# Unread matmuls on TensorE between the last down quarters of each layer and ahead of layer 1's first norm

## The chip, the cores and the metric

The kernel runs on one core of a Trainium2 chip. The metric is the time of one execution on the device in microseconds. Three runs of the kernel before gave 1234.24, 1233.4 and 1233.99 us, median 1233.99.

## The reference

A trunk of two decoder layers over 256 tokens of width 1024, all in float32. Layer 0 mixes tokens with retention and HGRN2, layer 1 with stick-breaking and differential attention. Behind each mixer stands a mixture of experts with two levels of routing.

```python
for l in range(DEPTH):
    h = rms_norm(x, norm_mix[l])
    if l % 2 == 0:
        mix = retention_hgrn2_mixer(h, w_in_ab[j], w_out_ab[j], ...)
    else:
        mix = stickbreak_diff_mixer(h, w_in_cd[j], w_out_cd[j], ...)
    x = x + mix
    h = rms_norm(x, norm_ffn[l])
    x = x + hierarchical_moe(h, ..., w_gate[l], w_up[l], w_down[l])

def expert_block(args):          # 32 experts a layer, top 2 for each token
    xb, e = args
    a = jax.nn.silu(xb @ w_gate[e]) * (xb @ w_up[e])
    return a @ w_down[e]
```

## The kernel before, in words

Every engine runs a program of its own, written out by hand, and they meet at semaphores. SyncE (SP) issues the loads. Weights come in units of 2 MB (128 partitions x 4096 floats) into eleven places, six in `ring` and five in `wide`. A place is loaded again when TensorE has counted up `unit_used` for the unit that lay there, so SP follows TensorE by that one counter.

A layer's mixer projects the normed input with `w_in` (`project`, L759 with a 512 wide moving operand, L756 with a 256 wide one), attends, and multiplies by `w_out` (L806). Ahead of layer 1's mixer TensorE transposes the normed tokens (`turn_h`, L701, 8 transposes for each half of the tokens), VectorE and ScalarE copy them to `hT` (L735), and the first projection begins.

The experts of a layer are worked through in 8 quads of 4 experts. A quad has three matrices, gate, up and down, four units each, and `matrix` (L531) multiplies them: four experts stand side by side in the array, each with 32 columns of weights (the tokens that chose it), and 512 columns of expert weights stream past. A float32 matmul leaves two records in the trace. In between, `gather` (L487) picks the tokens of the next quad, and `spread_back` (L494, 4 matmuls, 8 records) adds the outputs of the quad before to the sums in PSUM banks 0 to 3. The last down matrix of a layer (quad 7, matrix 2) is loaded in another cut: its four units are quarters, unit q holding chunk q of all four experts, and TensorE waits for a quarter (`wait_unit`), does its 8 matmuls, and goes to the next. The order on TensorE at a layer's end is thus: the last up matrix, the transposes L558 and L560, four quarters of down, and, after VectorE and ScalarE have copied the result out (L640, L592), the last `spread_back`. VectorE adds it to `x` (L643). Then every engine looks at a flag (`over_i`, L835 on TensorE) for whether some expert had more tokens than its 32 slots, and branches; with these inputs that work is passed over.

Behind layer 0, ScalarE squares `x` (L673), VectorE finds the root (L655 to L658) and applies the norm (L689, one instruction for each half of the tokens), and TensorE's transposes for layer 1 wait for each half. Bank 5 of PSUM, `UP`, holds the product with the up matrix, and later the turned weights that ScalarE copies to `spread` (L590).

Of the kernel before, what the change touches and what calls it, by code (L numbers as in the profile page):

```python
# [24 lines left out]
SEQ = 256  # L25
# [104 lines left out]
def build(nc, t, where, const_width, stop_after=4):  # L130
    with ExitStack() as ctx:
# [16 lines left out]
        psum = ctx.enter_context(nc.psum_tensor("psum", [P, 8, 512], F32))  # L148
# [15 lines left out]
        def const(name):  # L164
            a, b = where[name]
            if b <= KEPT_CONSTS:
                return consts[:, a:b]
            tables, start = (masks0, KEPT_CONSTS) if b <= LAYER1_CONSTS else (masks1, LAYER1_CONSTS)
            return tables[:, a - start:b - start]

        ident, before, from_on = const("ident"), const("before"), const("from_on")
        ones = const("ones")
# [94 lines left out]
        def moe_base(layer):  # L267
            return unit_base(layer) + UNITS_IN[layer] + UNITS_OUT

        def unit_place(layer, n):  # L270

            l, m, place = in_turn[unit_base(layer) + n]
            assert (l, m) == (layer, n)
            return place

        def expert_unit(layer, u):

            return UNITS_IN[layer] + UNITS_OUT + u
# [6 lines left out]
        def unit_landings(layer, n):  # L285

            place = unit_place(layer, n)
            return 16 * sum(in_turn[i][2] == place for i in range(unit_base(layer) + n + 1))
# [5 lines left out]
        def slot(layer, n):  # L294

            place = unit_place(layer, n)
            return ring[:, place, :] if place < RING else wide[:, (place - RING) * UNIT:(place - RING + 1) * UNIT]

        def group_buffer(b):

            return ring[:, 2 * b:2 * b + 2, :].rearrange("p u (h n) -> p (u h) n", n=HALF)

        def wait_unit(eng, layer, n):
            eng.wait_ge(unit_landed[unit_place(layer, n)], unit_landings(layer, n))
# [158 lines left out]
        ACC, GATE, UP, YB = 0, 4, 5, 6  # L463
# [8 lines left out]
        def start_sums(pe, layer, rnd):  # L472

            pe.wait_ge(M[layer]["y_ready"], 2 * (rnd * (QUADS + 1) + 1))
            for b in range(4):
                pe.matmul(psum[:, ACC + b, :], spread[:, 0, :], y_sb[:, 0:512], start=True, stop=False,  # L476
                          skip_group_check=True)

        def moe_pe(pe, layer, over, rnd):
            m = M[layer]  # L480
            n17, n16 = rnd * (QUADS + 1), rnd * QUADS
            mb = moe_base(layer)

            def gather(chunks=KC):
                for c in range(chunks):
                    for tc in range(TC):
                        mm = pe.matmul(psum[:, YB + c // 4, (c % 4) * P:(c % 4 + 1) * P], h[:, tc, c, :],  # L487
                                       sel[:, tc, :], start=tc == 0, stop=tc == TC - 1)
                mm.then_inc(m["gathered"], 1)

            def spread_back():
                for tc in range(TC):
                    for n in range(2):
                        mm = pe.matmul(psum[:, ACC + 2 * tc + n, :], spread[:, tc, :],  # L494
                                       y_sb[:, 512 * n:512 * (n + 1)], start=False, stop=False,
                                       skip_group_check=True)
                mm.then_inc(m["spread_done"], 1)

            def over_matrix(i, matrix, out, inp, rows, width):

                for j in range(2):
                    b = (2 * matrix + j) % OVER_BUFFERS
                    pe.wait_ge(over_landed[layer, b], (((rnd - 1) * QUADS + i) * (GROUPS // OVER_BUFFERS)
                                                       + ((2 * matrix + j) // OVER_BUFFERS + 1)) * 16)
                    w = group_buffer(b).rearrange("p e (c n) -> p e c n", n=width)
                    for k in range(rows // 2):
                        c = j * (rows // 2) + k
                        for n in range(width // 512):
                            for e in range(TILE):
                                slots = slice(e * SLOTS, (e + 1) * SLOTS)  # L510
                                mm = pe.matmul(psum[slots, out + n, :], inp[:, c, slots], w[:, e, k, 512 * n:512 * (n + 1)],
                                               start=c == 0, stop=c == rows - 1)
                    mm.then_inc(m["used"], 1)

            def matrix(i, matrix, out, inp, rows, width):

                if over:
                    return over_matrix(i, matrix, out, inp, rows, width)
                units = [expert_unit(layer, i * PER_QUAD + matrix * TILE + j) for j in range(TILE)]
                quartered = (i, matrix) in QUARTERED  # L520
                per = rows // 4
                for c in range(rows):
                    if quartered and c % per == 0:
                        wait_unit(pe, layer, units[c // per])
                    for n in range(width // 512):
                        for e in range(TILE):
                            if not quartered and c == 0 and n == 0:
                                wait_unit(pe, layer, units[e])
                            slots = slice(e * SLOTS, (e + 1) * SLOTS)
                            unit, at = (units[c // per], (e * per + c % per) * width) if quartered else (units[e], c * width)  # L530
                            mm = pe.matmul(psum[slots, out + n, :], inp[:, c, slots],  # L531
                                           slot(layer, unit)[:, at + 512 * n:at + 512 * (n + 1)],
                                           start=c == 0, stop=c == rows - 1)
                            if not quartered and c == rows - 1 and n == width // 512 - 1:
                                mm.then_inc(S["unit_used"], 1)
                    if quartered and (c + 1) % per == 0:
                        mm.then_inc(S["unit_used"], 1)

            if over:
                start_sums(pe, layer, rnd)  # L540
            pe.wait_ge(m["sel_ready"], n17 + 1)
            pe.wait_ge(S["normed"], TC * (2 * layer + 2))
            gather()
            if not over:
                pe.wait_ge(S["route_ready"], layer + 1)

            def quad(i, last=False):
                pe.wait_ge(m["xT_ready"], n17 + i + 1)
                matrix(i, 0, GATE, xT, KC, FF)
                pe.wait_ge(m["y_ready"], 2 * (n17 + i + 1))  # L550
                spread_back()
                matrix(i, 1, UP, xT, KC, FF)

                pe.wait_ge(m["sel_ready"], n17 + i + 2)
                gather(1 if last else KC)
                pe.wait_ge(m["act_ready"], n16 + i + 1)
                for c in range(FC):
                    pe.transpose(psum[:, GATE, c * P:(c + 1) * P], act_h[:, c, :], ident)  # L558
                for tc in range(TC):
                    mm = pe.transpose(psum[:, UP, tc * P:(tc + 1) * P], selw[:, tc, :], ident)  # L560
                mm.then_inc(m["turned"], 1)
                pe.wait_ge(m["actT_ready"], n16 + i + 1)
                pe.wait_ge(m["xT_ready"], n17 + i + 2)
                matrix(i, 2, YB, actT, FC, D)
            if over:
                with pe.Fori(0, QUADS) as i:
                    quad(i)
            else:
                for i in range(QUADS):
                    quad(i, last=i == QUADS - 1)  # L570
            pe.wait_ge(m["y_ready"], 2 * (n17 + QUADS + 1))
            spread_back()

        def moe_act(act, layer, over, rnd):
            m = M[layer]
# [1050 lines left out]
```

## Time and profile before

| | |
|---|---|
| median of three runs | 1233.99 us |
| profiled execution | 1239.58 us, span 1237.8 us |
| TensorE (PE) busy | 957.2 us, 77% of the span |
| VectorE (DVE) busy | 244.8 us, 20% |
| ScalarE (ACT) busy | 133.0 us, 11% |
| read from HBM | 446.47 MB, 362 GB/s over the span |
| mean granted TensorE clock | 0.879 of full speed |

The table is of one profiled execution. It shows no engine busy all the time; what bounds a stretch has to be read from the stretch itself. The granted clock is given as a share of full speed: 1.00 is 2.4 GHz and 0.50 is 1.2 GHz.

### The profile page before, as it was taken

How to read it: one execution, taken by the hardware profiler on the slowest of the kernel's cores; microseconds unless marked ns; L12 is line 12 of the kernel's file. 1: busy time of each engine (PE TensorE's matmuls, PEld its weight loads, DVE VectorE, ACT ScalarE, POOL GpSimd, SP SyncE). 2: the span in 40 equal slices, each digit the busy share in tenths (PEclk: the TensorE clock that was granted, in tenths of full speed). 3: DMA queues.
4: the chain of work that ended last, by engine and by line, in shares of the span. 5: the costliest groups of instructions: out<-in, count | busy, mean ns of one | idle time of the engine just before them, and what ended most of it. 6: DMA issues, size and time to landing. Idle time of an engine off the chain costs nothing.

```text
span 1237.8 us, 11947 instructions
## 1 busy us (share of the span) xinstructions
PE 957.2 (77%) x5092; PEld 403.6 (33%) x5092; DVE 244.8 (20%) x664; ACT 133.0 (11%) x228; POOL 9.9 (1%) x10
## 2 busy tenths in 40 slices
PE   5999999776776858576759999896767677585775
PEld 4645554221212212131225755532121212121211
DVE  3622333110101010110134441511000000010101
ACT  3401211000000000000011331110000000000000
POOL 0000010000000000000000000000000000000000
PEclk9999999987878878787979999998788788887878
DMA  9773396999999999999995327799999999999994
GB/s 325 242 264 134 143 429 279 429 429 426 428 428 427 426 430 427 428 428 426 412 387 188 126 79 281 317 428 429 429 425 429 427 429 427 428 427 429 426 421 196
DMA packets 62149, 448.32 MB, mean 362 GB/s; under 512 B 13072, under 2 KB 13328, under 8 KB 39568
## 3 DMA queue, kind: packets, MB, share of 16 engines
q1 hardware_dynamic: 62096, 447.53, 87.5%
q8 instruction: 43, 0.70, 0.2%
q14 instruction: 10, 0.08, 0.0%
HBM read 446.47 MB, written 1.05 MB: 362 GB/s over the span
## 4 chain that ended last, share of the span: by engine, by line
DMA 50%; PE 45%; DVE 2%; SPq 1%; issue 1%; ACT 1%; DVEq 0%; ACTq 0%
PE psum L531 17%; DMA ring<-in_w_up 15%; PE psum L759 11%; DMA ring<-in_w_down 10%; DMA wide<-in_w_gate 10%; DMA wide<-in_w_down 9%; DMA ring<-in_w_gate 5%; PE psum L756 5%; PE psum L806 4%; PE psum L487 1%; PE psum L494 1%; PE psum L476 1%; SPq L337 1%; PE psum L701 1%; DMA x<-in_x 0%
## 5 line engine op out<-in xcount | busy, mean ns | idle before, releaser
L531 PE MATMUL psum<-ring,mixed 128*32 128x512 f32 x1664 | 400.7, 704 | 128.2 <-DMA ring<-in_w_up 57.2
L531 PE MATMUL psum<-wide,mixed 128*32 128x512 f32 x1408 | 402.8, 721 | 110.8 <-DMA wide<-in_w_gate 61.4
L531 PEld LDWEIGHTS psum<-ring,mixed 128*32 128x32 f32 x1664 | 92.1, 127 | 331.4 <-issue 162.0
L531 PEld LDWEIGHTS psum<-wide,mixed 128*32 128x32 f32 x1408 | 88.5, 129 | 273.7 <-issue 120.3
L759 PE MATMUL psum<-ring,wide 128*128 128x512 f32 x320 | 142.3, 600 | 1.3 <-DVE wide L735 1.3
L759 PEld LDWEIGHTS psum<-ring,wide 128*128 128x128 f32 x320 | 60.4, 193 | 72.0 <-issue 70.2
L635 DVE TENSOR_TENSOR mixed<-psum,sig 128x512 f32<-128x512 f32 x16 | 16.9, 1057 | 279.2 <-PE psum L531 279.2
L494 PE MATMUL psum<-y_sb,spread 128*128 128x512 f32 x144 | 66.6, 605 | 1.6 <-DVE y_sb L640 1.6
L487 PE MATMUL psum<-sel,h 128*128 128x128 f32 x520 | 62.8, 279 | 3.5 <-DVE sel L608 3.5
L487 PEld LDWEIGHTS psum<-sel,h 128*128 128x128 f32 x520 | 59.4, 192 | 17.1 <-issue 13.4
L756 PE MATMUL psum<-wide,ring 128*128 128x256 f32 x256 | 59.7, 395 | 1.4 <-DVE wide L735 1.4
L632 DVE TENSOR_TENSOR sig<-psum,sig 128x512 f32<-128x512 f32 x16 | 11.1, 691 | 238.4 <-ACT sig L585 238.4
L579 ACT COPY mixed<-psum 128x1024 f32<-128x1024 f32 x18 | 18.2, 1012 | 354.9 <-PE psum L487 354.9
L756 PEld LDWEIGHTS psum<-wide,ring 128*128 128x128 f32 x256 | 50.2, 198 | 10.1 <-DVE wide L735 1.8
L640 DVE COPY y_sb<-psum 128x512 f32<-128x512 f32 x16 | 11.1, 691 | 197.9 <-PE psum L531 197.9
L616 DVE TENSOR_SCALAR selw<-consts,rank,wtab 128x32 f32<-128x32 f32 x144 | 31.4, 295 | 50.6 <-PE psum L560 50.5
L494 PEld LDWEIGHTS psum<-y_sb,spread 128*128 128x128 f32 x144 | 25.9, 189 | 43.7 <-issue 39.2
L585 ACT ACTIVATE sig<-psum 128x512 f32<-128x512 f32 x16 | 9.6, 597 | 254.7 <-PE psum L531 254.7
L592 ACT COPY y_sb<-psum 128x512 f32<-128x512 f32 x16 | 9.4, 585 | 210.1 <-PE psum L531 210.1
L608 DVE TENSOR_SCALAR sel<-consts,rank,small 128x32 f32<-128x32 f32 x144 | 31.3, 294 | 0.1
L806 PE MATMUL psum<-ring,y_sb 128*128 128x512 f32 x64 | 28.4, 594 | 0.4 <-ACT small L1044 0.4
L806 PE MATMUL psum<-ring,wide 128*128 128x512 f32 x64 | 27.8, 592 | 0.0
(243 smaller groups left out, 468.4 us busy)
## 6 DMA issues: line engine op xcount, KB each, us to landing
ring<-in_w_down SPq DMA_DIRECT2D x38, 2048.0 KB, 34.8
ring<-in_w_up SPq DMA_DIRECT2D x36, 2048.0 KB, 38.3
wide<-in_w_gate SPq DMA_DIRECT2D x34, 2048.0 KB, 36.1
ring<-in_w_gate SPq DMA_DIRECT2D x30, 2048.0 KB, 30.8
wide<-in_w_up SPq DMA_DIRECT2D x28, 2048.0 KB, 28.3
wide<-in_w_down SPq DMA_DIRECT2D x26, 2048.0 KB, 35.5
ring<-in_w_in_ab SPq DMA_DIRECT2D x8, 2048.0 KB, 15.2
ring<-in_w_in_cd SPq DMA_DIRECT2D x6, 2048.0 KB, 20.4
```

Source lines behind the costliest of these rows:

```text
L337: sp.dma_start(dst_cols(slot(layer, n)), src).then_inc(unit_landed[unit_place(layer, n)], 16)
L476: pe.matmul(psum[:, ACC + b, :], spread[:, 0, :], y_sb[:, 0:512], start=True, stop=False, skip_group_check=True)
L487: mm = pe.matmul(psum[:, YB + c // 4, (c % 4) * P:(c % 4 + 1) * P], h[:, tc, c, :], sel[:, tc, :], start=tc == 0, stop=tc == TC - 1)
L494: mm = pe.matmul(psum[:, ACC + 2 * tc + n, :], spread[:, tc, :], y_sb[:, 512 * n:512 * (n + 1)], start=False, stop=False, skip_group_check ...
L531: mm = pe.matmul(psum[slots, out + n, :], inp[:, c, slots], slot(layer, unit)[:, at + 512 * n:at + 512 * (n + 1)], start=c == 0, stop=c == ...
L579: nc.scalar.copy(xT, psum[:, YB:YB + 2, :].rearrange("p b (c s) -> p (b c) s", s=P)).then_inc(m["xT_ready"], 1)
L608: r = nc.vector.tensor_scalar(sel[:, tc, e * SLOTS:(e + 1) * SLOTS], const("iota"), rank[:, tc, bass.ds(quad * TILE + e, 1)], small[:, 2 + ...
L616: r = nc.vector.tensor_scalar(selw[:, tc, e * SLOTS:(e + 1) * SLOTS], const("iota"), rank[:, tc, bass.ds(quad * TILE + e, 1)], wtab[:, tc, ...
L635: nc.vector.tensor_tensor(act_h.rearrange("p c s -> p s c"), psum[:, UP, :].rearrange("p (s c) -> p s c", c=FC), sig.rearrange("p (s c) -> ...
L756: mm = pe.matmul(banks[:, m // 2, (m % 2) * SEQ:(m % 2 + 1) * SEQ], w[:, c, m * P:(m + 1) * P], hT[:, c, :], start=c == 0, stop=c == KC - 1)
L759: mm = pe.matmul(banks[:, m, :], hT[:, c, m * P:(m + 1) * P], w[:, c, :], start=c == 0, stop=c == KC - 1)
L806: mm = pe.matmul(psum[:, OUT_BANK[layer] + 2 * tc + n, :], mixT(half)[:, c, tc * P:(tc + 1) * P], w[:, c, 512 * n:512 * (n + 1)], start=ha ...
```

## The change

A new function in `moe_pe`, `stay_warm(times)`, issues matmuls of the 128x128 identity with a 128x256 table of ones, into bank 5 (`UP`). Nothing reads what they write, and no semaphore stands on them. They are issued at two places:

- in `matrix`, for the last down matrix of a layer: 6 of them before the waits for quarters 1, 2 and 3, so 18 a layer, in both layers;
- in `moe_pe`, behind the last `spread_back` of layer 0: 20 of them, ahead of the look at the flag.

The first quarter of quad 0's gate matrix is cut in quarters too, but is excluded by `matrix == 2`.

```diff
+            def stay_warm(times):
+
+                for _ in range(times):
+                    pe.matmul(psum[:, UP, 0:SEQ], ident, ones, start=True, stop=True, skip_group_check=True)
+
             def over_matrix(i, matrix, out, inp, rows, width):
...
                     if quartered and c % per == 0:
+                        if matrix == 2 and c:
+                            stay_warm(6)
                         wait_unit(pe, layer, units[c // per])
...
             pe.wait_ge(m["y_ready"], 2 * (n17 + QUADS + 1))
             spread_back()
+            if layer == 0 and not over:
+                stay_warm(20)
```

TensorE's order at the end of layer 0 before, from the last transposes to the flag. `mixed` is the turned activation, the `wide` operand the down weights, and `unit_landed6` to `unit_landed9` are the landings of quarters 0 to 3:

```order
L560 MATMUL psum<-consts,selw 128x128 x2
L531 MATMUL psum<-wide,mixed 32x512 [waits unit_landed6,moe0_xT_ready,moe0_actT_ready]
L531 MATMUL psum<-wide,mixed 32x512 x7
L531 MATMUL psum<-wide,mixed 32x512 [waits unit_landed7]
L531 MATMUL psum<-wide,mixed 32x512 x7
L531 MATMUL psum<-wide,mixed 32x512 [waits unit_landed8]
L531 MATMUL psum<-wide,mixed 32x512 x7
L531 MATMUL psum<-wide,mixed 32x512 [waits unit_landed9]
L531 MATMUL psum<-wide,mixed 32x512 x7
L494 MATMUL psum<-y_sb,spread 128x512 [waits moe0_y_ready]
L494 MATMUL psum<-y_sb,spread 128x512 x3
```

And the same place now (the lines of the file have moved: L531 is L538, and L502 is the new matmul):

```order
L538 MATMUL psum<-wide,mixed 32x512 x7
L502 MATMUL psum<-consts 128x256 x6
L538 MATMUL psum<-wide,mixed 32x512 [waits unit_landed7]
L538 MATMUL psum<-wide,mixed 32x512 x7
L502 MATMUL psum<-consts 128x256 x6
L538 MATMUL psum<-wide,mixed 32x512 [waits unit_landed8]
L538 MATMUL psum<-wide,mixed 32x512 x7
L502 MATMUL psum<-consts 128x256 x6
L538 MATMUL psum<-wide,mixed 32x512 [waits unit_landed9]
L538 MATMUL psum<-wide,mixed 32x512 x7
L494 MATMUL psum<-y_sb,spread 128x512 [waits moe0_y_ready]
```

Each group of six now stands in TensorE's order between one quarter's matmuls and the next quarter's wait; nothing else changed place. Behind the last `spread_back` of layer 0 stands now, on TensorE, the group of 20 and then the read of the flag:

```order
L494 MATMUL psum<-y_sb,spread 128x512 x3
L502 MATMUL psum<-consts 128x256 x20
L844 TENSOR_LOAD over_i
L844 ISA x2
L844 COMPARE_AND_BRANCH
```

Before, the read of the flag came directly behind `spread_back`:

```order
L494 MATMUL psum<-y_sb,spread 128x512 [waits moe0_y_ready]
L494 MATMUL psum<-y_sb,spread 128x512 x3
L835 TENSOR_LOAD over_i
L835 ISA x2
L835 COMPARE_AND_BRANCH
```

The other engines' orders are as they were.

## Rows read from the trace of the kernel before

**Rows 1.** The page's chain that ended last: shares of the span by engine.

```profile
DMA 50%; PE 45%; DVE 2%; SPq 1%; issue 1%; ACT 1%; DVEq 0%; ACTq 0%
```

**Rows 2.** The chain in order of time: start us, us, what.

```profile
596.59 24.05 DMA wide<-in_w_down
...
641.93 1.24 DVE wide L735
```

**Rows 3.** Timeline of TensorE, end of layer 0: start us, us, group [idle before].

```profile
611.71 3.64 PE L531 MATMUL psum<-wide,mixed 128*32 128x512 f32 x32 [0.95 <-ACT spread L590]
615.56 1.92 PE L531 MATMUL psum<-wide,mixed 128*32 128x512 f32 x16 [0.21 <-DMA wide<-in_w_down]
620.68 3.38 PE L531 MATMUL psum<-wide,mixed 128*32 128x512 f32 x16 [3.20 <-DMA wide<-in_w_down]
624.89 3.70 PE L494 MATMUL psum<-y_sb,spread 128*128 128x512 f32 x8 [0.82 <-DVE y_sb L640]
638.10 3.79 PE L701 MATMUL psum<-consts,h 128*128 128x128 f32 x16 [9.51 <-DVE h L689]
643.21 2.08 PE L759 MATMUL psum<-ring,wide 128*128 128x512 f32 x2 [1.32 <-DVE wide L735]
```

**Rows 4.** Timeline of TensorE, end of layer 1: its four down quarters.

```profile
1212.61 3.64 PE L531 MATMUL psum<-wide,mixed 128*32 128x512 f32 x32 [0.95 <-ACT spread L590]
1216.67 1.92 PE L531 MATMUL psum<-wide,mixed 128*32 128x512 f32 x16 [0.42 <-DMA wide<-in_w_down]
1221.68 3.26 PE L531 MATMUL psum<-wide,mixed 128*32 128x512 f32 x16 [3.08 <-DMA wide<-in_w_down]
```

**Rows 5.** Windows of TensorE: from:to, us, busy (records), clock, DMA share, GB/s.

```profile
612.00:617.00 5.00, 4.79 (x48) 1.00 1.02 409
...
620.50:623.50 3.00, 2.82 (x16) 0.50 1.05 387
624.50:628.50 4.00, 3.61 (x8) 1.00 1.05 388
...
634.00:638.00 4.00, 0.00 (x0) 0.50 1.05 381
...
643.00:647.00 4.00, 3.79 (x5) 0.50 1.05 388
648.00:652.00 4.00, 4.00 (x11) 1.00 1.05 391
```

**Rows 6.** The chain in order of time: two stretches of projection at full clock.

```profile
77.56 13.73 PE psum L759 x32
...
673.97 13.82 PE psum L756 x64
```

**Rows 7.** Timeline of weight loads (PEld), start of layer 1's first projection.

```profile
646.78 0.34 PEld L759 LDWEIGHTS psum<-ring,wide 128*128 128x128 f32 x1 [0.52 <-issue]
647.61 0.19 PEld L759 LDWEIGHTS psum<-ring,wide 128*128 128x128 f32 x1 [0.49 <-issue]
```

**Rows 8.** Timeline of TensorE, where the weights go between 32 and 128 columns.

```profile
589.82 0.59 PE L531 MATMUL psum<-wide,mixed 128*32 128x512 f32 x1
590.35 3.70 PE L494 MATMUL psum<-y_sb,spread 128*128 128x512 f32 x8
...
593.98 1.05 PE L531 MATMUL psum<-ring,mixed 128*32 128x512 f32 x4
```

**Rows 9.** Timeline of VectorE, from the end of layer 0 to the norm.

```profile
632.17 0.06 DVE L1481 MEMSET small<- 128x1 f32 x1 [1.20 <-issue]
...
636.07 3.79 DVE L689 SCALAR_TENSOR_TENSOR h<-x,small,wide 128x1024 f32<-128x1024 f32 x2
```

**Rows 10.** Timeline of TensorE, behind layer 1's mixer: transposes and router.

```profile
778.19 1.09 PE L709 MATMUL psum<-consts,x 128*128 128x128 f32 x8 [0.44 <-DVE x L1216]
779.12 3.88 PE L821 MATMUL psum<-rw,wide 128*128 128x36 f32 x32
```

**Rows 11.** Windows of TensorE over the same place, columns as in Rows 5.

```profile
777.00:783.00 6.00, 5.52 (x47) 1.00 1.01 430
784.00:787.00 3.00, 3.00 (x4) 0.52 1.02 437
```

**Rows 12.** Waits of SP's queue from 640 to 850 us: us in total, times, longest.

```profile
SPq L337 <- PE psum L759: 64.7, 4, 20.0
```

## The prediction

> **What bounds the kernel now.** I read the chain that ended last first. Half of the span is DMA and 45% TensorE [rows 1]: the experts' weights stream, and the mixers and what lies between them are TensorE's. The change touches two kinds of place only, so I went along the chain to those. At the end of layer 0 it runs over the load of the last down quarter [rows 2], over that quarter's matmuls, and the same at the end of layer 1.
>
> Then the timeline of TensorE at these ends. Quarters 0 and 1 have landed when TensorE comes to them and run as one block of 32 records, quarter 2 waits 0.21 us, and only quarter 3 waits long, 3.20 us [rows 3]. Layer 1 ends in the same way, with waits of 0.42 and 3.08 us [rows 4]. The granted clock is 1.00 up to the end of quarter 2 and 0.50 in quarter 3, where TensorE had stood still before it; it is back at 1.00 for `spread_back` [rows 5]. So the half clock costs at an end the difference between a quarter of 3.38 or 3.26 us and one of 1.92 us, about 1.4 us, and nothing behind it.
>
> After layer 0's last `spread_back` TensorE stands still for 9.51 us, until the first half of the norm is there [rows 3]. The clock is down at 634 us, and is still down when the projection begins at 643.21 us; it rises near 647.6 us, where the weight loads go from 0.34 to 0.19 us [rows 5, 7].
>
> **The price of one unread matmul.** It has a 256 wide moving operand, as L756 has, whose 64 records take 13.82 us at full clock [rows 6]: 0.216 us a record, two records a matmul, so 0.432 us. Six are 2.59 us, eighteen 7.78, twenty 8.64.
>
> **The ends of the layers.** The point is where the six stand. They are done whether the next quarter has landed or not. Before quarters 1 and 2 there is next to nothing to wait for, so these twelve push everything back, and the wait before quarter 3 is only some 3 us long.
>
> Layer 0, from the start of quarter 0 at 611.71 us: a quarter's 16 records stream in four groups of 0.43 us (0.43 is the pitch of the 32 records of L759 in 13.73 us [rows 6]), 1.72 us, four quarters 6.88 us, with 0.2 us until the last is out (1.92 less 1.72), 7.08 us. The eighteen add 7.78 us. Each time the weights change between 32 and 128 columns there is a small loss: L494 starts 0.53 us after the record of L531 before it, where 0.43 is the pitch, so 0.10 us; and its eight records, streaming until 590.35 + 8 x 0.43 = 593.79 us, are followed by L531 at 593.98 us, so 0.19 us [rows 8]. Three groups in between make 3 x 0.29 = 0.87 us. Sum 15.73 us: quarter 3 ends at 627.44 us instead of 620.68 + 3.38 = 624.06 us. That is 3.38 us later. All quarters have landed long before their turn (quarter 3 at 620.68 us, its turn is 627.44 - 1.92 = 625.5 us), so the wait that is to be covered is gone, the clock stays up, and the end is late all the same, because TensorE's own queue is late now.
>
> Layer 1: 1212.61 + 15.73 = 1228.34 us against 1221.68 + 3.26 = 1224.94 us, 3.40 us later. Together +6.8 us. The bounds: with no loss at the switches +2.5 us an end, 5.0 in all; with the loss half as large again, 3.8 us an end, 7.6 in all. I take 6.8, since the rows have both directions of the switch.
>
> What waits behind: VectorE's and ScalarE's copies of the result (L640, L592), then `spread_back`, the addition to `x`, and in layer 0 the norm, in layer 1 the output. Nothing beside them hides it. Of SP's queue in layer 1's first half I looked at whom it waits for: TensorE's projections above all [rows 12], so its loads for the next experts move with TensorE, and a delay or a gain at layer 1's start goes through to the end. The first two units of layer 1 are in time: the loads run at 388 GB/s throughout [rows 5] and the second is needed a projection later (13.73 us [rows 6]).
>
> **The start of layer 1.** Taken in the times of before, the twenty begin when `spread_back` has streamed, 624.89 + 8 x 0.43 = 628.33 us, and are out at 636.97 us. The transposes can start at 638.10 us at the earliest. So they fit, with 1.1 us to spare. Behind them TensorE reads the flag and branches, which has cost VectorE 1.20 us [rows 9]; even if TensorE begins that only when it has run dry, it is ready at 638.2 us, and the 0.1 us is lost in the pause before the second half of the transposes, which waits for the norm until 636.07 + 3.79 = 639.9 us. So nothing is added here.
>
> What can be won: the second eight transposes at full clock take 1.09 us [rows 10], so end at 641.0 instead of 641.89 us, 0.9 us. The projection runs cold from 643.21 to 647.61 us, 4.40 us for about 5.2 records of 0.85 us, which at 0.43 us take 2.2 us: 2.2 us more. In all 3.1 us, if the clock is still up after the pause of 1.1 us, the transposes, the pause between their halves, and the copy of 1.24 us [rows 2]. The other end is 0: the clock falls in that stretch, and the projection is as cold as before.
>
> The nearest place is behind layer 1's mixer: two bursts of transposes with pauses and small router matmuls, 777 to 783 us, at 1.00 throughout, and then 0.52 in the window after a pause of one us [rows 10, 11]. So a stretch of transposes and pauses holds the clock for some time, but six us of thin work ended at the half clock. Ours, from 637.0 to about 642.3 us, is a little shorter, with nothing between the transposes. I take 2.2 us, between the 0 and the 3.1, nearer to the upper end because the clock did hold in the row as long as transposes were in it.
>
> The Trainium skill has a rule that speaks against this (TensorE: Matmul & The Clock Gate, Part 4: PE-mode transpose): the full clock does not engage for transposes, since they don't count as busy in the way that matmuls do. By it the twenty would buy nothing, and the sum would be 6.8. Against it stands the window from 777 us at 1.00 with sixteen transposes in or just ahead of it [rows 11], which it doesn't foresee unless the router's matmuls count; so I leave it as a rival.
>
> **Sum.** +6.8 - 2.2 = +4.6 us on the profiled execution's 1239.58 us, 1244.2 us. The profiled execution is 5.6 us above the median of the runs shown, 1233.99 us; I carry the difference over unchanged: 1238.6 us, 0.4% slower.
>
> **The rivals.**
>
> 1. The clock does not last until the projection. The fall in the row at 784 us speaks for it. At most the second transposes gain. +6.8 - 0 to 0.9: 1239.9 to 1240.8 us, say 1240.5. Slower too. The change then does not do what its second part says.
>
> 2. The overrun is about as large as the gain. The switches cost nothing, since weights may be loaded ahead of the quarter, and the full 3.1 us come in: +5.0 - 3.1 = +1.9 us, 1235.9 us. Or a matmul of the identity costs half the price, 0.216 us: eighteen are 3.89 us, quarter 3 ends at 611.71 + 7.08 + 3.89 + 0.87 = 623.55 us, 0.5 us early at each end, but then the twenty are out at 632.7 us, long before the norm, and win nothing: -1.0 us, 1233.0 us. For it speaks nothing in the rows but that these operands do not occur in them.
>
> 3. Faster. Without the profiler the last quarters land later in relation to TensorE, so that the eighteen lie in a wait that is longer. Every us of that takes one us from each overrun. With the full 3.1 us of layer 1 it decides from 3.1 us on: 6.8 - 2 x 3.1 - 3.1 = -2.5 us, 1231.5 us; and if quarter 3 is 4.8 us later, so that it is just in time for its turn at 625.5 us, the warm quarter saves 1.4 us at each end, 1228 us. Against it: the two ends agree with each other within 0.2 us in all their waits, [rows 3, 4], and the quarters' landings are 5.1 and 5.0 us apart in both, which is the rate of the loads.
>
> **How the numbers follow.** Overrun at both ends and a gain of 1 to 3.1 us (1237.7 to 1239.8 us): 0.55. Rival 1: 0.25. Rival 2: 0.14. Rival 3: 0.06. A change of this kernel can be told from none from about 0.2%, 2.5 us, on: the forecast and rival 1 are slower by more, with a little of the forecast's lower edge lost: slower 0.81; within 0.2% rival 2 and part of rival 3, 0.14; faster 0.05. The range reaches from below 1235.9 us, the case of free switches, to 1241.6, which is the dear switches (7.6) without a gain: 1235.5 to 1241.6 us.
>
> **What would show it.** At both ends TensorE should be busy from quarter 0 to quarter 3 with no wait for `wide<-in_w_down`, the clock at 1.00 throughout, quarter 3 at 1.92 us, and its end 15.7 us after quarter 0's start. L502 should have 112 records, those of a group 0.216 us apart. The idle time before the transposes of layer 1 should fall from 9.51 to about 1.1 us. In the projection the weight loads of 0.34 us should be gone (forecast) or about five (rival 1). If quarter 3 still waits for its load, or the records of L502 are closer than 0.2 us, the first term is wrong and the time falls towards 1233.

## The result and the profile after

The changed kernel takes 1246.24 us (median of four runs, 1244.9 to 1247.13) against 1233.7 us, ratio 1.0098 with a 95% interval of 1.0081 to 1.0114. It is slower by 12.5 us; 4.6 were forecast, and the time lies outside the range.

Between the two profiled executions there are only 5.3 us (1244.9 against 1239.58). The profile after is 1.3 us below the median of its own kernel's runs; the one of before, on which the prediction rests, was 5.6 us above the median of its runs. Part of that is seen in the chain of waits. This is the chain of after, in order of time (start us, us, what):

```profile
16.67 27.89 PE psum L765 x128
...
642.14 1.98 PE psum L710 x16
...
645.42 27.73 PE psum L768 x64
...
1230.34 0.70 DVE y_sb L649
```

The first projection of layer 0 took 27.89 us here and 30.93 us in the profile of before, though nothing was changed there. The absolute times of the two profiles therefore can't be set against each other; distances inside a stage can. TensorE's timeline at the end of layer 0 after, columns as in [rows 3]:

```profile
597.13 9.97 PE L538 MATMUL psum<-ring,mixed 128*32 128x512 f32 x58 [3.86 <-DMA ring<-in_w_up]
...
610.06 1.92 PE L538 MATMUL psum<-wide,mixed 128*32 128x512 f32 x16 [0.95 <-ACT spread L599]
611.91 2.86 PE L502 MATMUL psum<-consts 128*128 128x256 f32 x12
614.70 1.92 PE L538 MATMUL psum<-wide,mixed 128*32 128x512 f32 x16
...
623.98 1.92 PE L538 MATMUL psum<-wide,mixed 128*32 128x512 f32 x16
626.72 3.70 PE L494 MATMUL psum<-y_sb,spread 128*128 128x512 f32 x8 [0.81 <-DVE y_sb L649]
630.26 8.80 PE L502 MATMUL psum<-consts 128*128 128x256 f32 x40
642.14 1.97 PE L710 MATMUL psum<-consts,h 128*128 128x128 f32 x16 [3.09 <-DVE h L698]
645.42 14.86 PE L768 MATMUL psum<-ring,wide 128*128 128x512 f32 x34 [1.32 <-DVE wide L744]
```

The tail is what was forecast: no wait for a down quarter is left, a quarter is 1.92 us, and quarter 3 ends 623.98 + 1.92 - 610.06 = 15.84 us after quarter 0's start (forecast 15.73). Until VectorE copies the result, at 625.97 us, it is 15.91 us, and 15.92 in layer 1. The windows (from:to, us, busy, clock, DMA share, GB/s) answer [rows 5]:

```profile
610.00:626.00 16.00, 15.85 (x100) 1.00 1.04 394
...
639.00:642.00 3.00, 0.05 (x1) 1.00 1.05 383
642.50:645.00 2.50, 1.60 (x15) 1.00 1.05 386
645.50:649.00 3.50, 3.50 (x9) 1.00 1.03 384
```

The clock is up from quarter 0 to the projection, as intended (1.00 in the windows between these too). But before the transposes TensorE stands still for 3.09 us behind the last of the twenty, where 1.1 us was forecast. VectorE's own row says that it is TensorE that is late:

```profile
637.91 3.79 DVE L698 SCALAR_TENSOR_TENSOR h<-x,small,wide 128x1024 f32<-128x1024 f32 x2
```

The first half of the norm, for which the first transposes wait, was ready near 639.9 us, the second at 641.7, and the transposes began at 642.14.

So the profile after confirms the work at the tail and shows one cost that was not foreseen. It does not show where the other 7 us of the 12.5 come from. For that the kernel before had to be seen in a usual execution.

### The profile page after: what moved, and what is told of

The parts are those of the page before. It is cut to its first block, busy times and chain, and to the rows that moved or that the text cites. A ratio compares the mean times of both kernels' runs of the same rounds, so it can differ in the third digit from the quotient of the medians.

```text
span 1243.0 us, 12171 instructions
## 1 busy us (share of the span) xinstructions
PE 979.8 (79%) x5204; PEld 423.4 (34%) x5204; DVE 245.0 (20%) x664; ACT 133.1 (11%) x228; POOL 9.9 (1%) x10
## 4 chain that ended last, share of the span: by engine, by line
DMA 48%; PE 47%; DVE 3%; issue 1%; ACT 1%; DVEq 0%; ACTq 0%
PE psum L538 18%; DMA ring<-in_w_up 13%; PE psum L768 11%; DMA wide<-in_w_gate 10%; DMA wide<-in_w_down 10%; DMA ring<-in_w_down 5%; DMA ring<-in_w_gate 5%; DMA wide<-in_w_up 5%; PE psum L765 5%; PE psum L815 4%; PE psum L502 1%; PE psum L487 1%; PE psum L494 1%; PE psum L476 1%; DVE h L698 0%
## 5 line engine op out<-in xcount | busy, mean ns | idle before, releaser
L538 PE MATMUL psum<-ring,mixed 128*32 128x512 f32 x1664 | 407.2, 715 | 123.2 <-DMA ring<-in_w_up 53.1
L538 PE MATMUL psum<-wide,mixed 128*32 128x512 f32 x1408 | 402.4, 712 | 105.1 <-DMA wide<-in_w_gate 62.9
L538 PEld LDWEIGHTS psum<-ring,mixed 128*32 128x32 f32 x1664 | 92.9, 128 | 326.0 <-issue 161.2
L538 PEld LDWEIGHTS psum<-wide,mixed 128*32 128x32 f32 x1408 | 88.2, 127 | 267.3 <-issue 122.3
L765 PE MATMUL psum<-wide,ring 128*128 128x256 f32 x256 | 56.7, 381 | 1.4 <-DVE wide L744 1.4
## 6 DMA issues: line engine op xcount, KB each, us to landing
ring<-in_w_gate SPq DMA_DIRECT2D x30, 2048.0 KB, 30.9
```

What stands on the lines that cost most here:

```text
L538: mm = pe.matmul(psum[slots, out + n, :], inp[:, c, slots], slot(layer, unit)[:, at + 512 * n:at + 512 * (n + 1)], start=c == 0, stop=c == ...
L765: mm = pe.matmul(banks[:, m // 2, (m % 2) * SEQ:(m % 2 + 1) * SEQ], w[:, c, m * P:(m + 1) * P], hT[:, c, :], start=c == 0, stop=c == KC - 1)
```

## The experiments

Ratios are to the kernel before, whose median was 1233.1 to 1233.7 us in these comparisons; behind each stands its 95% interval. A diff that takes out or alters `stay_warm` is against the changed kernel, one that adds a loop of matmuls is against the kernel before, and the last one against the run with twelve and fourteen. "To the copy" is the distance from the start of down quarter 0 to VectorE's copy of the result (L640).

### The kernel before, seen again

> The kernel before, unchanged, as a second profile of it. The profiled execution of before (1239.58 us) lay 5.6 us above its timed runs, while that of after (1244.9) lay at the lower edge of its runs. Theory P (the clock's phase): the granted clock rises and falls at other moments of the program from one execution to the next, and the first profile of before met an unlucky start (clock up at 22.9 us, 3 us of extra time in the first projection). Then this profile is near 1234 us, with the projection L756 x128 in the chain near 28 us instead of 30.93, and the last up matrices of 8.5 or 9.9 us depending on where the rise falls. Theory S: the profiled execution is slower by itself; then 1239 to 1240 again with 30.9 us there. Ratio 1.000 either way.

Measured: 1232.22 us, 0.9998 (0.9976 to 1.0019), profile 1235.91 us. First the last up matrix in the first profile, from its second block on, which [rows 3] leaves out:

```profile
600.24 8.51 PE L531 MATMUL psum<-ring,mixed 128*32 128x512 f32 x58 [3.85 <-DMA ring<-in_w_up]
```

And the timeline of TensorE at the ends of layer 0 and, in the last line, of layer 1 in the second profile:

```profile
601.81 9.70 PE L531 MATMUL psum<-ring,mixed 128*32 128x512 f32 x58 [3.87 <-DMA ring<-in_w_up]
...
614.46 5.36 PE L531 MATMUL psum<-wide,mixed 128*32 128x512 f32 x48 [0.95 <-ACT spread L590]
622.26 1.92 PE L531 MATMUL psum<-wide,mixed 128*32 128x512 f32 x16 [2.44 <-DMA wide<-in_w_down]
625.00 3.70 PE L494 MATMUL psum<-y_sb,spread 128*128 128x512 f32 x8 [0.81 <-DVE y_sb L640]
638.21 3.52 PE L701 MATMUL psum<-consts,h 128*128 128x128 f32 x16 [9.51 <-DVE h L689]
643.05 3.27 PE L759 MATMUL psum<-ring,wide 128*128 128x512 f32 x7 [1.32 <-DVE wide L735]
...
1219.29 1.92 PE L531 MATMUL psum<-wide,mixed 128*32 128x512 f32 x16 [2.28 <-DMA wide<-in_w_down]
```

Set beside [rows 3] three things differ. Quarter 3 runs at full clock, 1.92 us instead of 3.38. The last up matrix's second block takes 9.70 us, where it took 8.51 in the first profile: more of it is at the half clock, so quarter 0 starts later in relation to the loads and the copy is reached 9.80 us after it, not 12.43. And the projection of layer 1 is warm without any unread matmuls. The windows show the clock:

```profile
602.00:606.00 4.00, 4.00 (x20) 0.50 1.03 410
...
620.00:622.00 2.00, 0.00 (x0) 1.00 1.04 397
622.50:626.00 3.50, 2.69 (x19) 1.00 1.05 389
634.00:637.00 3.00, 0.00 (x0) 0.50 1.05 384
...
638.00:641.00 3.00, 2.79 (x13) 0.50 1.05 386
641.00:642.00 1.00, 0.73 (x5) 0.85 1.05 385
642.00:643.00 1.00, 0.00 (x0) 1.00 1.06 391
643.00:647.00 4.00, 3.95 (x9) 1.00 1.05 386
```

From the up matrix's second block to the landing of quarter 3 it is 622.26 - 601.81 = 20.45 us here and 620.68 - 600.24 = 20.44 us in the first profile. The loads set that, not TensorE. A slower up matrix comes out of the wait for quarter 3, and behind the shorter wait the clock is still up. Layer 1's end is alike (9.64 us to the copy). The sixteen transposes begin at 0.50 behind 9.51 us of standing still, and the clock rises within them (0.85 in the window from 641 us), so that the projection finds it up; in the first profile the same transposes stayed at 0.50.

The first projection took 29.52 us in the chain, between the expected values. Theory P holds: two executions of one program differ in where the clock changes. Theory S falls: of the fourteen profiled executions of this document six lie below the median of their kernel's runs, by 1.2 to 3.6 us.

> The kernel before, unchanged, one more look, to see how often its last quarter runs cold. In its first profile it took 3.38 and 3.26 us behind a wait of 3.2 us, in the second 1.92 us at both ends behind a wait of 2 us, after a last up matrix of 9.6 to 9.8 us instead of 8.4. Theory A (the time that a half clock costs in the last up matrix comes out of the wait for quarter 3, so from up's second block to the landing of quarter 3 there are always 20.4 us): again 20.4 us, and either a short up with a cold quarter or a long up with a warm one. If the first profile was typical: both ends 12.4 us from quarter 0 to the copy.

Measured: one profile, 1236.26 us. 20.45 us again in layer 0 and 20.92 in layer 1, the up block 9.80 and 9.92 us, quarter 3 1.92 us at both ends, 9.67 and 10.04 us to the copy. Over all nine profiles of kernels without unread matmuls at the tails there are 18 layer ends. In 15 the up block took 9.6 to 10.0 us, the wait before quarter 3 was 2.0 to 2.7 us and the quarter 1.92 us. In 3 the up block took 8.35 to 8.51 us, the wait was 3.1 to 3.2 us and the quarter was cold; two of these are the first profile's. From up's second block to the landing it is 20.3 to 20.5 us in 17 of the 18, and why it was 20.92 once is open.

### The tails alone

In all four of these the twenty are left out.

```diff
-            if layer == 0 and not over:
-                stay_warm(20)
```

> Only the three groups of six unread matmuls before quarters 1, 2, 3 at both layers' ends; the twenty are left out. My sum: +3.4 to 3.5 us at each end. Layer 1's start as before (transposes and projection cold). So +7 us, 1241 us. Rival (the twenty cost the rest): the same +7 here, and the twenty add 5. Rival (the tails cost more in the timed runs than in the profile, because the quarters land earlier or the clock never fell there): +9 to +12 here.

Measured: 1245.71 us, 1.0102 (1.0069 to 1.0135), 12 us slower; 15.92 us to the copy at both ends. The last rival is met: the tails are the loss of 12.5 us to within the noise. The distance from the up matrix's second block to the copy shows how: in the second profile of before it is 22.45 and 22.44 us, after the change 625.97 - 597.13 = 28.84 and 1230.34 - 1201.70 = 28.64 us, with the tails alone 28.62 and 28.86. For the change that is 6.4 and 6.2 us, together 12.6.

```diff
-                            stay_warm(6)
+                            stay_warm(3)
```

> The three groups, but three unread matmuls in each instead of six, both layers' ends, without the twenty. Theory A: quarter 0 to the copy is 15.92 - 9 x 0.432 = 12.0 us, against 9.7 us: +2.3 us an end, +4.6 us in all, 1238 us. My prediction's rows, with a cold last quarter (12.4 us from quarter 0 to the copy): -0.4 an end, -0.8 us in all.

Measured: 1239.57 us, 1.0051 (1.0032 to 1.0071), and 12.03 us to the copy at both ends, as theory A has it to 0.03 us. The loss falls with the number of unread matmuls: 6.2 to 6.4 us an end with eighteen, about 2.3 with nine. In the timed runs it is 6.3 us (3.9 to 8.8), where theory A's 4.6 lies inside the interval. By the first profile's 12.43 us nine would have been free; the time says that they are not.

```diff
-                        if matrix == 2 and c:
+                        if matrix == 2 and c == 3:
```

> Six unread matmuls before quarter 3 alone, at both layers' ends; nothing else added. The wait there is 3.1 to 3.2 us, six take 2.8 us with the switches: they fit, the last quarter should run at the full clock, 1.92 us instead of 3.3, the end 1.4 us earlier in each layer: -2.8 us, 1231 us. If the clock was not down there in the timed runs: 0. If the six overrun even here: +0.5 an end.

Measured: 1234.34 us, 1.0009 (0.9995 to 1.0022). The 2.8 us are not there; quarter 3 is warm, but it was so already in the second profile of before. To the copy it takes 10.07 us at both ends: the six with their switches are 0.3 to 0.4 us longer than the wait of that profile.

```diff
-                        if matrix == 2 and c:
+                        if matrix == 2 and c == 1:
```

> Six unread matmuls before quarter 1 alone, where there is no wait at all, at both layers' ends. Theory A (only TensorE's total between quarter 0 and the landing of quarter 3 counts; the end is the later of the landing + 2.0 us and of quarter 0 + the sum of the work): the same as six before quarter 3, from quarter 0 to the copy of the result 10.0 to 10.2 us, against 9.7 in the second profile of before; +0.5 to +1 us in all. Theory B (six hurt where nothing is waited for and are hidden where 2 us are): 2.8 us later at each end than six before quarter 3, so +6 us.

Measured: 1235.86 us, 1.0018 (1.0003 to 1.0033), and the same 10.07 us to the copy. The place of the six makes no difference to that distance. Theory A holds and B falls: the 6 us it asks for are outside the interval. In the distances of all these runs the end is the later of two things, the landing of quarter 3 plus 2.0 us and the sum of TensorE's work from quarter 0 on.

### The twenty

None of these three has unread matmuls at the tails. The first has the twenty of the change, the second ten in their place, and the third none there but fourteen behind the branch.

```diff
-                        if matrix == 2 and c:
-                            stay_warm(6)
```

> Only the twenty unread matmuls behind the last spread_back of layer 0. By the profile of after, TensorE comes 2.2 us late to layer 1's transposes (they start 3.2 us after the last of the twenty), and wins 1.8 us in the transposes and 2.2 us in the projection: -1.8 us, 1232 us. My prediction had no lateness here: -3.1 to 0. Rival (the twenty are what the timed runs pay for): slower, +3 to +6 us.

Measured: 1235.93 us, 1.0022 (1.0004 to 1.0039), profile 1237.29 us. Not a gain. The transposes begin 16.26 us after the copy of layer 0's result, where before has 13.95 or 13.96 us in all three profiles, and in this execution the clock fell all the same:

```profile
626.19 8.80 PE L502 MATMUL psum<-consts 128*128 128x256 f32 x40
...
638.16 2.79 PE L708 MATMUL psum<-consts,h 128*128 128x128 f32 x16 [3.18 <-DVE h L696]
642.26 3.78 PE L766 MATMUL psum<-ring,wide 128*128 128x512 f32 x4 [1.32 <-DVE wide L742]
```

Four records in 3.78 us are at the half clock. The granted clock is 1.00 from 638 to 639 us, 0.57 from 639 to 640 and 0.50 from there to 644 us: it fell within the transposes, 2.79 us in all, where the profile after has 1.97. From the copy to the end of the first projection block it is 49.9 us, against 46.5 in the second profile of before. So whether the twenty carry the clock into the projection differs from one execution to the next, and the 2.3 us of lateness are paid in both.

```diff
-                stay_warm(20)
+                stay_warm(10)
```

> Nothing at the tails, and ten unread matmuls ahead of the flag where the change has twenty. Theory A (the flag is read only when TensorE's queue has run dry, and the read with the branch takes 3.1 to 3.5 us): the ten end 4.3 us sooner than the twenty, the branch is done before the norm's first half, and the transposes start 13.95 us after the copy of layer 0's result, as in before, against 16.2 to 16.3 with twenty. The clock has 4.3 us more of standing still, so it may fall again; 0 to -2 us, 1232 to 1233 us. Theory B (the lateness has another cause): still 2 us late.

Measured: 1233.19 us, 0.9999 (0.9987 to 1.0011). The transposes are back at 13.95 us after the copy, so the lateness is a matter of when the queue runs dry; they begin cold again, 3.48 us, and the projection is warm. No gain, no loss. (One of its ten runs took 3738 us; there is no profile of it, its cause is open, and it is not in the ratio.)

```diff
+            for _ in range(14):
+                pe.matmul(psum[:, UP, 0:SEQ], ident, ones, start=True, stop=True, skip_group_check=True)
             turn_h(pe, 2)
```

> Nothing at the tails. Fourteen unread matmuls stand behind the read of the flag and its branch, directly ahead of layer 1's transposes, instead of twenty ahead of the flag. Theory A (with the twenty ahead, TensorE reads the flag only when its queue has run dry, which costs 3.1 us and makes the transposes 2.3 us late): now they start 13.95 us after the copy of layer 0's result, as before, unless the fourteen overrun (6.05 us from about 3 us after spread_back, so up to the norm's first half), and take 2 us instead of 3.5: -1.5 us, and the projection is warm in every execution: -1 us more on average; 1231 us. Theory B (the lateness comes from the unread matmuls themselves, however they stand): transposes 2 to 3 us late here too, +1 us or more.

Measured: 1236.75 us, 1.0031 (1.0018 to 1.0045), slower. The timeline has the flag's price by itself, in front of the fourteen:

```profile
623.07 3.70 PE L494 MATMUL psum<-y_sb,spread 128*128 128x512 f32 x8 [0.81 <-DVE y_sb L640]
630.26 9.19 PE L913 MATMUL psum<-consts 128*128 128x256 f32 x28 [3.49 <-issue]
639.29 1.91 PE L701 MATMUL psum<-consts,h 128*128 128x128 f32 x16
```

3.49 us pass between `spread_back` and the first matmul behind the branch, with nothing to wait for. In that time the clock falls in this execution, so the fourteen take 9.19 us instead of some 6, and overrun the norm: 16.97 us from the copy to the transposes, which is as late as theory B had it, by another cause. The expected gain was wrong, the price of the branch right. What part of the 3.49 us is the read of the flag and what the branch is not shown.

### Where unread matmuls could pay

With the fourteen, and ahead of layer 0's first transposes:

```diff
+            for _ in range(12):
+                pe.matmul(psum[:, UP, 0:P], ident, ident, start=True, stop=True, skip_group_check=True)
             turn_h(pe, 0)
```

> As the run with fourteen behind the flag, and besides twelve unread 128x128 matmuls ahead of layer 0's first transposes, where TensorE waits 11.6 us for the first norm. They need the first constants, landed near 6 us, and take 5.2 us at half clock or less. If the clock rises before the transposes (11.6 us): these take 2 us instead of 3.7, and the first projection 27.8 us instead of 27.9 to 30.9: -2 to -4 us against the run with fourteen alone, 1228 us. If it does not rise with this work: no change against that run. If they overrun: up to +0.5.

Measured: 1234.73 us, 1.0008 (0.9991 to 1.0025). By the medians it is 2 us better than the fourteen alone, in line with the estimate for layer 0, though the two intervals overlap, and no better than the kernel before. In its profile the clock stayed at 1.00 over the 3.46 us of the branch: there the fourteen took 6.31 us, and the transposes began 14.05 us after the copy, only 0.1 us late. That the fourteen ran cold in most of its other runs is likely and not shown.

> Only the twelve unread 128x128 matmuls ahead of layer 0's first transposes; nothing at layer 1 and at the tails. In the profile of the run with both the clock was up from the first transposes (2.3 instead of 3.7 us of them, projection 27.9 instead of 27.9 to 30.9 us). So -1.5 to -4 us, 1230.5 us, and no cost, since no flag stands there and they end at 11.66 us, where the norm is ready at 11.64. If nothing is won: 1233 us.

The edit is the twelve of the diff above alone. Measured: 1232.53 us, 0.9988 (0.9972 to 1.0003): a trend, not clear of zero. Its profile has the first experts at 191.93 us, as have the other two with the twelve (191.98 and 191.92). The three profiles of before have them at 195.74 to 197.07, but of the eight other profiles of kernels that are unchanged up to there four have them at 192.6 to 192.8. So against the best of the others 0.7 us is gained, and whether the twelve also narrow the scatter, which goes up to 5 us, three profiles don't show.

```diff
-            for _ in range(14):
+            for _ in range(7):
```

> Twelve unread 128x128 matmuls ahead of layer 0's first transposes as in the run before, and seven 256 wide ones behind the flag's branch ahead of layer 1's (fourteen overran the norm by 3 us when they ran at the half clock; seven take 3.0 us at the full and 6.0 us at the half clock, and 6 us are free). The transposes of layer 1 start 13.95 us after the copy of layer 0's result. -2 to -4 us from layer 0 and 0 to -2 us from layer 1: 1229 to 1231 us. If the clock's scatter elsewhere takes it all back: 1233.

Measured with both the twelve and the seven: 1231.46 us, 0.9985 (0.9975 to 0.9994). This version beats both kernels, the one before by less than 0.2%. What the seven add to the twelve, 1.1 us by the medians, is not clear of the noise. The seven end where the norm is ready, and the transposes are warm:

```profile
626.83 6.05 PE L915 MATMUL psum<-consts 128*128 128x256 f32 x14 [3.50 <-issue]
632.87 1.09 PE L701 MATMUL psum<-consts,h 128*128 128x128 f32 x8
634.69 1.09 PE L701 MATMUL psum<-consts,h 128*128 128x128 f32 x8 [0.72 <-DVE h L689]
637.10 8.42 PE L759 MATMUL psum<-ring,wide 128*128 128x512 f32 x19 [1.32 <-DVE wide L735]
```

## Why the prediction was wrong

- **What was right:** the direction, and the mechanism of the overrun. No wait was left at the tails, the clock stayed up, and quarter 3 ended 15.84 and 15.85 us behind quarter 0's start (forecast 15.73; the switches were 0.13 and 0.20 us, not 0.10 and 0.19).
- **The step that failed: the ends of the layers, +6.8 us, where 12.6 was right.** What was wrong is what the new tail was set against: "quarter 3 ends at 627.44 us instead of 620.68 + 3.38 = 624.06 us". The 3.38 us of a cold quarter and the 9.0 us from quarter 0 to its landing both came from one execution, in which the up matrix had happened to run mostly at the full clock and the last quarter at the half one. In the usual execution it is the other way round: in the second profile of before quarter 0 starts 1.2 and 1.4 us later in relation to the landing of quarter 3, the wait is 2.4 and 2.3 us, and the quarter is warm. The two errors have the same sign: 1.4 us of cold quarter that was not there to be saved, and 1.2 to 1.4 us less between quarter 0 and the landing. To the copy it was 9.80 and 9.64 us, not 12.43 and 12.41: 2.6 and 2.8 us, 5.4 in all. With 0.2 us for the work itself and 0.2 us because the up blocks were not of the same length in the two profiles compared, 6.8 becomes 12.6.
- The timed runs leave no trace. That their tails are like those of the usual profiles is argued from their times: the tails alone cost 8.5 to 16.7 us (95% interval) and the threes 3.9 to 8.8, where the prediction's rows give 6.8 and -0.8.
- **The premise of the change falls with it.** At the tails there was mostly no half clock to be avoided. The bound from both sides that the prediction gave for this term (5.0 to 7.6 us) varied only the price of the switches; the quantity that varied in truth was not bounded at all. The signs under "What would show it" could not catch this: those for the tails came true, since they look at the new tail and not at what it is set against.
- **The argument from the place** (twelve of the eighteen stand where nothing is waited for) was beside the point: six before quarter 1 and six before quarter 3 reach the copy at the same 10.07 us. Only the sum counts.
- **The price of an unread matmul**, 0.432 us, was right: nine fewer gave 15.92 - 12.03 = 3.89 us, 0.432 each.
- **The start of layer 1, -2.2 us, was wrong in sign, if small.** From the copy of layer 0's result to the end of the first projection block it is 46.5 and 46.6 us in the two later profiles of before, 49.0 in the first, and 47.2 us after the change, 0.6 us longer. Two things failed. "So nothing is added here" took VectorE's 1.20 us for the flag; on TensorE it is 3.1 to 3.5 us, which made the transposes 2.2 us late. And the 2.2 us of a cold projection were mostly not there to be won: of eight profiles with no unread matmul at this place five have 46.5 to 46.8 us and three 49.0 to 49.8. What was won is 1.6 us of the transposes.
- **Rival 1** (the clock does not last) did not happen in the profile after, where it was 1.00 throughout, and did in the run with the twenty alone; it is open from one execution to the next. The rule that the prediction cites from the Trainium skill (TensorE: Matmul & The Clock Gate, Part 4: PE-mode transpose), that the full clock does not engage for transposes, is not borne out here. In the second profile of before the clock went from 0.50 to 1.00 while TensorE did sixteen transposes and nothing else, and the same is seen in the runs with the ten and with the twelve alone; in the first profile of before it stayed at 0.50.
- **Rival 3** supposed the last quarters late without the profiler. The truth was its mirror image: the wait was shorter than in the first profile, and each us went to the overrun.
- **Sum with the measured terms:** 6.4 + 6.2 at the tails, +0.6 at layer 1's start, 13.2 us, against 12.5 measured, interval 10.0 to 14.1. The two profiled executions, after and the second of before, differ by only 9.0 us (spans of 1243.0 and 1234.0): the one of after came to layer 0's last up matrix 4.7 us sooner, and nothing is changed up to there.
- The warning stood in the table: the profiled execution was 5.6 us above the median of the runs. The prediction carried that over "unchanged". Against the second profile of before, the first is longer by 1.4 us (up matrix to copy, layer 0), 1.3 us (the same, layer 1) and 2.4 us (copy to the end of layer 1's first projection block): 5.1 us in the very stages that the change touches, of which 1.6 us were made up before layer 0's last up matrix.
- A slip that changed nothing: the forecast and rival 1 have 0.80 between them, so "slower" could not have 0.81.

## What to carry to other kernels

Where a profiled execution is further from its median than the effect to be forecast, don't take a wait and a duration beside it from that one execution: take a second profile, ask which of the two gives way when the clock changes elsewhere, and bound the sum over both. Unread work in front of a wait was free here only up to the wait of the usual execution, not of the profiled one, and all of it counted against the one landing that the stage ends with, wherever it stood. Ahead of a branch such work must end earlier by the time that the branch takes, and that time has to be read for the engine itself: VectorE's was not TensorE's.

## What the runs showed of the hardware

- Reading a flag and branching took TensorE 3.1 to 3.5 us after its last matmul (3.09 and 3.18 us behind the twenty, 3.46 to 3.50 us in front of the fourteen and the seven), and VectorE 1.2 us. Before the change this lay unseen in the wait for the norm.
- The granted clock changes at other moments in executions of programs that are the same up to that place: first projection 27.9 to 30.9 us, last up block of layer 0 8.4 to 10.0 us, last quarter 1.92 or 3.3 to 3.4 us. Timed runs of the kernel before spread over 1231 to 1242 us. Some of it cancels, since an up matrix that is 1.2 us longer shortens the way from quarter 0 to the landing of quarter 3 by as much.
- In eight profiles TensorE comes to layer 1's sixteen transposes from 9.51 us of standing still, at a granted clock of 0.50. In five the projection behind them runs at the full clock from its start (27.73 us for 64 records), in three it does not (29.9 to 30.8 us). So the transposes did not keep the clock down, but whether it is up behind them differs from one execution to the next.
- Of that scatter not all was traced. Why the long up matrix with the warm quarter is so much more frequent (15 of 18) than its opposite stays open.
